# Input projection of a hybrid encoder layer by seven block products, with k in two halves whose partial tiles are added in DRAM

## The reference

```
h = rmsnorm(x, norm_w)
proj = h @ w_in[0]                         # 1024 x 2048 @ 2048 x 8208
q_a, k_a, v_a, z_a, q_m, k_m, v_m, o_m, z_m, g = split(proj)
# group A: 8 heads x 128, softmax attention over three dilated windows, q and k
#          normalised, the first 32 dims rotated; times silu(z_a)
# group B: 4 heads, qk 128, v 256, bidirectional mLSTM in chunks, own norm;
#          times sigmoid(o_m) and silu(z_m)
y = concatenate([attn, hm])                # 1024 x 2048
out = x + y @ w_out[0]                     # 2048 x 2048
```

## Time and profile before

| | us |
|---|---|
| median of 3 runs (2256.12 to 2256.47) | 2256.23 |
| span of the profiled execution | 2249.3 |
| busy: PE, weight load, DVE, ACT, POOL | 2202.3, 1815.7, 880.3, 528.5, 81.0 |
| moved by DMA | 131.48 MB, 58 GB/s over the span |

### The profile page before, as it was taken

The page is one execution under the profiler, slowest core; times in us unless marked ns, Lnnn a source line. Parts: engine busy times, 40 slices in busy tenths (PEclk is TensorE's granted clock), DMA queues, the critical chain, the costliest instruction groups (busy, mean ns, idle before and its releaser), DMA issues.

```text
span 2249.3 us, 28336 instructions
## 1 busy us (share of the span) xinstructions
PE 2202.3 (98%) x10432; PEld 1815.7 (81%) x10432; DVE 880.3 (39%) x1975; ACT 528.5 (23%) x899; POOL 81.0 (4%) x137
## 2 busy tenths in 40 slices
PE   5999999999999999999999999999999999999998
PEld 4788888888888888888888878888887887888886
DVE  7524432442344134344544454454445325111211
ACT  5212321331223123212222221322223214111110
POOL 4000000000000000000000000000000000000000
PEclk9999999999999999999999999999999999999999
DMA  5111121112111111211111111111111323323321
GB/s 195 39 47 38 38 61 43 38 42 62 43 34 62 47 38 38 88 43 38 37 42 33 47 28 51 34 43 39 37 43 29 117 79 112 108 86 105 102 87 44
DMA packets 59819, 131.48 MB, mean 58 GB/s; under 512 B 7136, under 2 KB 7392, under 8 KB 59616
## 3 DMA queue, kind: packets, MB, share of 16 engines
q1 hardware_dynamic: 49680, 93.56, 14.2%
q0 software_dynamic: 10064, 36.90, 4.5%
HBM read 113.66 MB, written 16.78 MB: 58 GB/s over the span
## 4 chain that ended last, share of the span: by engine, by line
PE 97%; DVE 2%; ACT 1%; issue 0%; DMA 0%; SPq 0%; POOL 0%; DVEq 0%; ACTq 0%
PE ps L289 26%; PE ps L291 26%; PE ps L290 26%; PE ps L492 2%; PE ps L463 2%; PE ps L318 2%; PE ps L324 1%; PE ps L444 1%; PE ps L390 1%; PE ps L399 1%; PE ps L393 1%; PE ps L496 1%; PE ps L466 1%; PE ps L377 1%; PE ps L494 1%; PE ps L464 0%
## 5 line engine op out<-in xcount | busy, mean ns | idle before, releaser
L289 PE MATMUL ps<-h_hi,w_hi 128*128 128x512 f32 x2592 | 1035.0, 399 | 31.8 <-DVE w_lo L271 12.9
L291 PE MATMUL ps<-h_hi,w_lo 128*128 128x512 f32 x2592 | 1014.8, 392 | 0.0
L290 PE MATMUL ps<-h_lo,w_hi 128*128 128x512 f32 x2592 | 1013.0, 391 | 0.7 <-issue 0.7
L289 PEld LDWEIGHTS ps<-h_hi,w_hi 128*128 128x128 f32 x2592 | 489.6, 189 | 130.6 <-issue 18.2
L291 PEld LDWEIGHTS ps<-h_hi,w_lo 128*128 128x128 f32 x2592 | 489.0, 189 | 105.4 <-issue 1.1
L290 PEld LDWEIGHTS ps<-h_lo,w_hi 128*128 128x128 f32 x2592 | 490.3, 189 | 95.1
L271 DVE TENSOR_TENSOR w_lo<-w_raw,w_hi 128x512 fp32r<-128x512 f32 x324 | 230.0, 710 | 524.6 <-ACT w_hi L266 518.9
L266 ACT CAST w_hi<-w_raw 128x512 fp32r<-128x512 f32 x324 | 199.7, 617 | 826.1 <-PE ps L291 826.0
L620 ACT ACTIVATE arena<-arena 128x128 f32<-128x128 f32 x64 | 25.7, 402 | 319.1 <-DVE arena L913 319.0
L687 ACT ACTIVATE arena<-arena,small 128x704 f32<-128x704 f32 x64 | 56.6, 884 | 167.7 <-DVE small L1064 167.7
L821 DVE SCALAR_TENSOR_TENSOR arena<-ps,xrs 128x512 f32<-128x512 f32 x80 | 55.1, 690 | 99.3 <-PE ps L291 99.3
(11 more groups left out here) (156 smaller groups left out, 1461.1 us busy)
## 6 DMA issues: line engine op xcount, KB each, us to landing
w_raw<-w_all_dram SPq DMA_DIRECT2D x324, 256.0 KB, 2.6
x_raw<-xT_dram SPq DMA_DIRECT2D x16, 512.0 KB, 10.0
arena<-y_dram POOLq DMA_DIRECT2D x16, 512.0 KB, 3.6
arena<-xT_dram POOLq DMA_DIRECT2D x16, 512.0 KB, 5.7
outT_dram<-arena POOLq DMA_DIRECT2D x16, 512.0 KB, 4.4
y_dram<-arena POOLq DMA_DIRECT2D x4, 1024.0 KB, 5.4
y_dram<-arena POOLq DMA_DIRECT2D x8, 512.0 KB, 3.2
arena<-rope_dram POOLq DMA_DIRECT2D x16, 128.0 KB, 2.6
```

What stands on the lines that cost most here:

```text
L289: nc.tensor.matmul(psP[:, i, :], hi, h_hi[:, kt, cols], start=kt == 0, stop=False)
L290: nc.tensor.matmul(psP[:, i, :], hi, h_lo[:, kt, cols], start=False, stop=False)
L291: mm = nc.tensor.matmul(psP[:, i, :], lo, h_hi[:, kt, cols], start=False, stop=kt == KT - 1)
```

## The change

The 64 tiles of 128 columns that are the input projection without the gates become 32 pairs of tiles, and each pair is computed by Strassen's scheme in Winograd's form. The blocks are: two tiles of columns, two blocks of k of 512, two halves of the tokens. Seven products take the place of eight. As a pair has k = 2048 and the scheme covers 1024 (two blocks of 512), each pair is done in two halves of k, as two groups: 64 groups of 7 products, each of 12 matmuls of 128 by 512 (4 k-tiles by 3). In the code a unit `u` is one product; 448 units for the input, then 128 units of 12 matmuls for the output projection, which stays as it was in arithmetic but runs in two halves of k, the first half's sums stored to `part` in DRAM and added again later.

- The moving side of the products is not h but seven sums of blocks of it, `t_hi` and `t_lo` [7 x 4 x 512], built for one half of k at a time: at the start for the first half, twice more for groups 16 and 48. A build loads 4 MB of x again; ACT scales it (`scale_x`) and rounds (`t_high`, 2048 elements a row), DVE does `t_one`, `t_two` and `t_low`, POOL does `t_three` and `t_four`. They use the arena of the heads, so they lie where no head does.
- The standing side: four of the seven blocks are sums of weight blocks (`s_one` to `s_four`), 128 by 512, on DVE, from the four loaded blocks of the group. All seven are split like before: 448 roundings on ACT and 448 subtractions on DVE for the input, where there were 256.
- Each product is read out when it is done: two of seven by ACT, five of seven by DVE, added to what is kept in six buffers `xt`; some products add up in the same bank. PE waits for the read-out of the product two before it.
- The four tiles of a group (128 by 512) are stored to `fin` in DRAM. The second group of a pair adds its tiles to the first one's by an accumulating DMA, which POOL issues (128 of them); plain stores are SP's (128).
- The heads read their tiles back from `fin` (SP), and scale them by the token's norm factor themselves: POOL for o_m, z_m, v_a, z_a (1024 elements a row, 4 for each mLSTM head and 2 for each attention head), DVE for v_m, and q and k of the attention in their own norm.
- The gates and the norm have a stream of their own in units 8 to 41: x again in 16 k-tiles, ACT rounds and squares, DVE subtracts, POOL adds the squares, PE does four matmuls for each k-tile instead of six. The sum over the partitions is one row of 8 small matmuls, not eight rows.
- A head of the mLSTM takes 49 units (a step every second one), a head of attention 18 units and starts the next before its own last units; the last three heads of attention lie in the output projection, whose first half of k needs the mLSTM alone. y is split a tile at a time, ahead of its use. No loop of the program is left: all units are written out.

```diff
+PRODUCTS = 7
+GROUPS = ([(p, 0) for p in range(M_PAIRS)]
+          + [(4 * j + i if i < 4 else M_PAIRS + 3 * j + i - 4, 1)
+             for j in range(M_HEADS) for i in range(7 if j < 3 else 11)]
+          + [(M_PAIRS + p, 0) for p in range(A_PAIRS)])
+STAGE = (0, M_PAIRS, NG - A_PAIRS)
+IN_UNITS = PRODUCTS * NG
+A_START = [357 + 18 * h for h in range(ATT_HEADS)]
+BUILD_AT = [None] + [PRODUCTS * (g - 1) for g in STAGE[1:]]
...
+            def product(u):
+                g, n = divmod(u, PRODUCTS)
+                bank = u % 2
+                pe.wait_ge(lo_done, u + 1)
+                if n == 0 and g >= 1:
+                    pe.wait_ge(ev_d, 5 * (g - 1) + 4)
...
+                if n == 2:
+                    pe.wait_ge(ev_a, 2 * g + 1)
...
+                new = n in (0, 1, 4)
+                for k in range(KP):
...
+                    nc.tensor.matmul(ps[:, bank, :], hi, t_hi[:, n, k, :], start=new and k == 0, stop=False,
+                                     skip_group_check=True)
...
+            def evict(u):
+                g, n = divmod(u, PRODUCTS)
+                if n in (0, 2):
+                    return
+                dve.wait_ge(prod, u + 1)
...
+                if n == 3:
+                    if g >= 1:
+                        stored(dve, X3, g - 1)
+                    nc.vector.tensor_tensor(x3, bank, x1, ALU.add).then_inc(ev_d, 1)
...
+            def s_one(g):
...
+                nc.vector.tensor_tensor(s_tmp[:, 0, :], w_raw[:, 0, :], w_raw[:, 1 + g % 2, :], ALU.add
+                                        ).then_inc(s_done, 1)
...
+            def t_low(b, n):
+                dve.wait_ge(th_done[n], t_made(n, b))
...
+                nc.vector.tensor_tensor(t_lo[:, n], t_src[n], t_hi[:, n].bitcast(F32), ALU.subtract
+                                        ).then_inc(tl_done[n], 1)
...
+            def build(b, off):
+                if off == -1:
+                    t_one(b)
+                if off == 2:
+                    t_two(b)
+                if off in (1, 3, 4, 5, 6, 8, 9):
+                    t_low(b, {1: 0, 3: 2, 4: 1, 5: 3, 6: 4, 8: 6, 9: 5}[off])
...
+            for u in range(UNITS):
+                if 1 <= u <= IN_UNITS:
+                    evict(u - 1)
+                if prepared_in(u) is not None:
+                    weight_lo(prepared_in(u))
+                if u < IN_UNITS:
+                    g, n = divmod(u, PRODUCTS)
+                    if n == 0:
+                        s_three(g)
+                    if n == 2:
+                        s_four(g)
+                    if n == 3 and g + 1 < NG:
+                        s_one(g + 1)
+                    if n == 5 and g + 1 < NG:
+                        s_two(g + 1)
...
+                gates_and_norm(u)
+                for b in (1, 2):
+                    build(b, u - BUILD_AT[b])
+                for j in range(M_HEADS):
+                    mlstm_dve(j, u - M_START[j])
+                for h in range(ATT_HEADS):
+                    attention_dve(h, u - A_START[h])
...
+            def t_three(b, kt):
+                pool.wait_ge(t1_done, 4 * b + kt + 1)
+                pool.wait_ge(pre[B22], 4 * b + kt + 1)
+                nc.gpsimd.tensor_tensor(stage[B12][:, kt, :], stage[B22][:, kt, :], stage[B12][:, kt, :], ALU.subtract
+                                        ).then_inc(t3_done, 1)
...
+            def added(g, n):
+                if n == 0 and g >= 1 and accumulated(g - 1):
+                    store_c21(pool, g - 1, xa, accum_op=ALU.add)
...
+            def mlstm_loads(j, at):
+                g = M_FINAL[j]
+                if at == 10:
...
+                    tile_done(sp, g[0], 0)
+                    sp.dma_start(halves(vst[0]), fin_tile(g[0], 0)).then_inc(v_in[0], 16)
```

More of the change, by code:

```diff
@@ new lines, in out_product @@
+            def out_product(u):
+                v = u - IN_UNITS
+                b = IN_UNITS + v // 2
+                piece, half = v % 4 // 2, v % 2
+                e = v // 4 * 2 + half
+                pe.wait_ge(lo_done, b + 1)
+                if piece == 0:
+                    if e >= 2:
+                        pe.wait_ge(o_done, e - 1)
+                    else:
+                        pe.wait_ge(ev_d, 5 * NG - 1 + half)
+                cols = slice(half * HALF, (half + 1) * HALF)
+                for k in range(KP):
+                    y = v // (O_UNITS // 2) * ATT_HEADS + piece * KP + k
+                    if v % (O_UNITS // 2) < 4 and half == 0:
+                        pe.wait_ge(y_lo, y + 1)
+                    hi = w_hi[:, b % 3, k * P:(k + 1) * P]
+                    lo = w_lo[:, b % 3, k * P:(k + 1) * P]
+                    yh = y_part(y, t_hi, y_late_hi)[:, cols]
+                    yl = y_part(y, t_lo, y_late_lo)[:, cols]
+                    nc.tensor.matmul(ps[:, half, :], hi, yh, start=piece == 0 and k == 0, stop=False)
+                    nc.tensor.matmul(ps[:, half, :], hi, yl, start=False, stop=False)
+                    mm = nc.tensor.matmul(ps[:, half, :], lo, yh, start=False, stop=piece == 1 and k == KP - 1)
+                mm.then_inc(prod, 1)
@@ L396, in step_products @@
                 pe.wait_ge(m_kw, 16 * j + n + 1)
-                if first and (n > 0 or not isinstance(j, int) or j > 0):
+                if first and 16 * j + n > 0:
                     pe.wait_ge(m_c, 16 * j + n)
@@ L435, in _ @@
[L435 to L450 removed]
+                    pe.wait_ge(m_y, 2 * j + 1)
@@ new lines, in square_sums @@
+            def square_sums(h):
+                pe.wait_ge(a_sq, 2 * h + 2)
+                if h > 0:
+                    pe.wait_ge(a_m, 8 * h)
+                else:
+                    pe.wait_ge(m_h, 16 * M_HEADS)
+                    pe.wait_ge(m_c, 16 * M_HEADS)
+                for i, src in enumerate((a_q, a_k)):
+                    for b in range(TB):
+                        mm = nc.tensor.matmul(ps[:, 4, i * TB + b:i * TB + b + 1], src[:, b * P:(b + 1) * P],
+                                              ones[:, 0:1], start=True, stop=True)
+                mm.then_inc(a_ss, 1)
@@ L1208, in _, with y_low @@
-            for i in range(2):
-                for s in range(PIECES if i == 0 else PIECES - LEAD):
-                    ahead((O_TILE + 2 * last + i, s))
-                output(O_TILE + 2 * last + i, i, last, False)
+                if 0 <= at - 11 < 8:
+                    masked(h, at - 11)
+            def y_low(k):
+                dve.wait_ge(y_hi, k + 1)
+                nc.vector.tensor_tensor(y_part(k, t_lo, y_late_lo), y_ring(k), y_part(k, t_hi, y_late_hi).bitcast(F32),
+                                        ALU.subtract).then_inc(y_lo, 1)
```

1885 lines of the change are left out of this document (1096 added, 789 removed).

## The result

The changed kernel takes 2205.93 us (median; 2199.45 to 2208.42) where the kernel before takes 2256.18: a ratio of 0.9774 [0.9759, 0.9789], 2.3% faster. I had said 2100, with 2055 to 2175. The direction is right, the size is not: of 156 us forecast, 50 came. The profiled execution took 2204.6 us, with a span of 2202.8, which stands against the 2249.3 of the earlier trace rows. So 1.8 us lie around the span, and in the other executions of the kernel before it is 1.5 to 1.6; of the 6.9 us between its median and its span, which I had put down to what lies around the span, the larger part is that this execution was faster than the median.

A forecast was written before the change was run, and what follows sets the result against it. PE's own matmul stream was taken as the bound: 2256.2 - 205.0 = 2051.2 us, plus 20 (builds), 9 (start), 6 (gates), 16 (heads), less 2 (tail), made 2100.2, so 2100 us, range 2055 to 2175.

The forecast's parts named there:

- The work removed: On PE: 800 fewer matmuls, -181.1 us; seven fewer rows of sums of squares, -12.6 us; waits gone, -11.3 us.
- The mLSTM heads: mLSTM: the chain in odd units holds, but POOL's scalings and the switch of heads cost 2 us a head, +7 us.
- The start: Start of the kernel: PE waits for DVE's first build and then runs slow matmuls, +9 us (0 to 13).
- The gate stream: Gates and the rows after: DVE and POOL need 6.9 us against PE's 6.3 in 16 pairs of units, +6 us.
- The tail: End of the kernel: 256 KB and not 512 KB left at the end, -2 us.
- The builds: Units around groups 16 and 48: DVE's work and POOL's additions outlast PE's 29.9 us, +20 us for both.
- The attention heads: Attention, units 6 to 10: rotations load DVE, 19 against 16 us; 1 us a head, +9 us with overlapping heads.
- DMA: Stores and loads of partial tiles: traffic rises to about 270 MB, accumulating stores land in time, 0 us.
- (a): Rival: the cover holds everywhere, builds cost 6 and the start 0: 2055 us; chance 0.2.
- (d): Rival: accumulating stores land late and hold heads' loads and read-outs; all gain lost at about 18 us each; chance 0.06.
- (c): Rival: each product's handover costs PE 0.2 us, 576 of them 115 us, giving 2215 us; chance 0.05.
- (b): Rival: POOL's lock on DVE sets the pace in heads, gates and builds: 2170 us; chance 0.17, from 2125 up.

The follow-up runs named there:

- three causes off: Changed kernel with attention's values one unit earlier, POOL's scalings of v and z cut to one column and rotations to 32 columns: 2114.0 us.

## Why the prediction was wrong, step by step

The whole difference on the span is about 110 us: my terms, made against the profiled execution, would have given 2093, and it came to 2203.

- **The work removed was right.** A unit of 12 took 2.72 us in the output. An mLSTM head took (1073.0 - 568.8) / 3 = 168.1 us by L1017, where I had 167.8 before losses. The root of each norm, in the mLSTM and then in attention (first and last start behind the durations):

```profile
L1017 ACT ACTIVATE m_rt<-m_sq,vec x4: 302/302/303, 568.8 to 1073.0; 128x8 f32<-128x8 f32 x4
```

```profile
L1061 ACT ACTIVATE qk_rms<-qk_arg x8: 215/215/216, 1215.2 to 1904.9; 128x16 f32<-128x16 f32 x8
```

PE's busy time is 2072.4 us where the matmuls removed would have left 2008.6 (2202.3 - 181.1 - 12.6). Of these 64 us the lower clock accounts for some 44 (57 against 13); no matmuls were added.

- **The mLSTM heads**, +7: measured +1 over the four by the same row, with 6.7 us idle in the whole stretch.
- **The start**, +9, which I worked out as 25 to 37 us behind PE's work, and 3 to 5 more: the first seven units took 45 us for 19 of PE and began at 12, 38 behind in all. **The gate stream**, +6: PE was idle for 3.3 us between the start and the first build. **The tail**, -2: the last matmul stands 3.6 us before the end of the span, before it was some 11: -7.5. The first two held, and the tail gave 5 us more than I had said.
- **The builds**, +20: measured 32 above the products. The step holds in kind (both engines' work was named, and the waits for L1209 are there). The sizes of the operations were a little low: `t_low` of 2048 took 2285 ns in the median, where I had 2200, and POOL's additions of 512 took 1712 and 1734, where I had halved to 1440 (durations are least, median and most; the 9.5 us are at the start, beside DVE's work). What I had not priced at all is the clock of 0.93 and 0.91, some 8 of the 12 us that are missing.

```profile
L1209 DVE TENSOR_TENSOR t_lo<-arena,t_hi x19: 2277/2285/3375, 28.3 to 1157.8; 128x2048 fp32r<-128x2048 f32 x19
...
L1607 POOL TENSOR_TENSOR arena<-arena x12: 1258/1712/9483, 16.9 to 1120.0; 128x512 f32<-128x512 f32 x12
...
L1613 POOL TENSOR_TENSOR arena<-arena x12: 1280/1734/3335, 32.1 to 1141.0; 128x512 f32<-128x512 f32 x12
```

- **The attention heads, +9, are the step that failed: +123.** By L1061 a head took (1904.9 - 1215.2) / 7 = 98.5 us where I had 83.3 and one more. The prediction said: "units 6 to 10 have rotations (2.4 a unit on top of 1.4, with POOL's scaling in them) and no attention work on PE: 19 against 16 us, with 2.7 of slack: 1 us a head". The bunch was found and counted as an amount of work against an amount of time, over the wrong stretch and with a slip. Five units of products are 13.6 us, so that the 16 holds the 2.7 of slack already, and 19 against 16 is 3 us a head, not 1. And the count began at unit 6: in units 4 and 5 DVE has the two norms of q and k, 2.0 us each. From unit 4 to 9 DVE has some 26 us of work against some 20 of PE with the slack in it, an estimate by the rows above, which is 48 us in eight heads; the run with small rotations gave 51. Three more things were not in it. The lock holds DVE for up to 2.8 us at the point at which slack is least, and in two places a head, not one. The values' new turn puts a PE to ACT to PE round trip into a unit of 2.72 us, for which the sum had no term; moving them back took 46 us off. And the clock fell, behind the row of one-column matmuls and behind long waits: some 40 us, for which I had a price at the start and nowhere else. My upper bound of 60 for the heads was less than half of what they lost.
- **DMA, 0**: about right. 262 MB moved and 119 GB/s, where I had about 270 and 130; plain stores gave nothing that can be told from the noise.
- **The rivals.** (a) and (d) are out by the runs. (c) is out by the output's 2.72 us a unit and by the mLSTM head's 168.1 us for 49 units of the input. Its 2215 is nearest to the 2206 measured, and that is luck. (b) gave 2170 and had one of the causes right: POOL's scalings did cost 35 us in attention, and I had put the chance that half of them show at 0.17. Its sign, subtractions with a mean well over 0.75 us, did not show (744 and 727 ns); a few held operations hardly move a mean of 512. It priced one cause of four, and the range ended with it.

What stays open: how the 123 us divide. Four cuts of 46, 16, 35 and 51 make 148. Since they overlap, no share of one cause alone can be given; only the total is. Open too is what decides whether the clock falls. It fell behind waits of 2.9 and 5.0 us in the changed kernel with nothing but products in the 8 us ahead of them, and it did not behind one of 3.1 us at 1335.68; of the rows of small matmuls some were followed by a fall and some were not.

## What to carry to other kernels

Where work moves from one engine to another, a share of busy time (72% here) says little: lay the moved work out unit by unit beside what already stands there, and ask of each unit which chain crosses engines and comes back within it. A step that is moved by one slot, with the same instructions, needs a price of its own, and the kernel before is the place to measure it. And a bound on losses should have the clock in it: where a change of slot took away 25 us of idle time, 17 us of the time in which PE worked went with it. Causes that are taken away one by one give a sum that cannot be banked: three gains of 132 together were 92.

## What I had not expected of the hardware

- PE's granted clock was 0.53 to 0.73 over the 6 us behind a row of 32 one-column matmuls in all eight heads of the changed kernel, with PE recorded as busy. A wait ahead of the row was not needed: with three causes off it fell behind the row in six heads without idle time in the 6 us ahead. Two rows of 16 in separate units had no fall behind the second, and one behind the first in five heads of eight.
- The clock also read 0.50 behind a wait of 2.94 us that had only product matmuls in the 11 us ahead of it, and stayed at 1.00 behind another of 3.14 us.
- The lock also held POOL: at the start its addition of 512 elements took 9.5 us, where its shortest took 1.26, while DVE worked from 16.1 to 25.2 us without a gap and at its usual 0.6 to 0.7 us an operation.
- Putting the 16 additions of 512 elements of the two builds from POOL onto the busier DVE shortened DVE's own busy time (43.1 to 40.4 us and 48.5 to 45.9).
- An accumulating store of 256 KB landed in 4.1 us, a plain one from the same queue in 2.3 (medians of 128).
